# Layer norm boundaries by token halves: last two product units, statistics and first two product units of the next matrix

## The reference, cut to what matters

```
h = layer_norm(x, ln_in_g, ln_in_b)
for l in range(2):
    proj = h @ w_in[l]
    ...
    mix = jnp.concatenate([o_a, o_b, o_c, o_d], axis=-1) @ w_out[l]
    h = layer_norm(DEEPNORM_ALPHA * h + mix, ln_mix_g[l], ln_mix_b[l])
    up = depthwise_conv(h @ ffn_w_up[l], ffn_conv_w[l], ffn_conv_b[l])
    f = (jax.nn.silu(up[..., :D_FF]) * up[..., D_FF:]) @ ffn_w_down[l]
    h = layer_norm(DEEPNORM_ALPHA * h + f, ln_ffn_g[l], ln_ffn_b[l])
return h

def layer_norm(x, g, b):
    mu = jnp.mean(x); var = jnp.mean((x - mu) ** 2)
    return (x - mu) * lax.rsqrt(var + 1e-5) * g + b
```

## Time and profile before

| | us |
|---|---|
| median of 3 runs | 2164.02 (2162.97 to 2166.41) |
| span of the profiled execution | 2162.8 |
| around the span, to the median | 1.2 |
| TensorE busy | 2072.4 (96%) |
| VectorE busy | 1186.1 (55%) |
| ScalarE busy | 786.0 (36%) |
| GpSimd busy | 176.5 (8%) |
| mean granted TensorE clock | 0.986 |

### The profile page before, as it was taken

The page is one execution under the profiler, slowest core; times in us unless marked ns, Lnnn a source line. Parts: engine busy times, 40 slices in busy tenths (PEclk is TensorE's granted clock), DMA queues, the critical chain, the costliest instruction groups (busy, mean ns, idle before and its releaser), DMA issues.

```text
span 2162.8 us, 24857 instructions
## 1 busy us (share of the span) xinstructions
PE 2072.4 (96%) x10090; PEld 1444.9 (67%) x10090; DVE 1186.1 (55%) x1798; ACT 786.0 (36%) x1199; POOL 176.5 (8%) x132
## 2 busy tenths in 40 slices
PE   6999999999999889889999999999999999999997
PEld 4787788843333333348657788888776677888885
DVE  6556534423333233366885864656677858646565
ACT  4546533312211111144673421222345734212233
POOL 1000000010000000000100110102001001101020
PEclk9999999999999999999999999999999999999999
DMA  5342243499999999942202222232222022222221
GB/s 193 117 150 75 78 175 116 157 359 408 406 408 400 398 410 415 421 153 79 72 1 78 90 95 97 87 101 98 96 100 71 2 78 96 95 97 87 101 95 52
DMA packets 41137, 357.61 MB, mean 165 GB/s; under 512 B 6320, under 2 KB 7512, under 8 KB 13376
## 3 DMA queue, kind: packets, MB, share of 16 engines
q1 hardware_dynamic: 36448, 342.99, 41.6%
q0 software_dynamic: 4288, 10.95, 1.7%
q10 hardware_dynamic: 288, 2.10, 0.2%
HBM read 354.94 MB, written 6.83 MB: 167 GB/s over the span
## 4 chain that ended last, share of the span: by engine, by line
PE 81%; DMA 9%; DVE 4%; ACT 3%; issue 2%; SPq 0%; DVEq 0%; ACTq 0%
PE bank L1103 40%; PE bank L2093 10%; PE bank L458 8%; DMA H<-in_expert_up_w 5%; PE bank L473 3%; PE bank L480 2%; DMA AUX<-in_expert_up_w 2%; DMA ring<-in_expert_up_w 2%; PE bank L1885 2%; PE bank L1870 1%; PE bank L1901 1%; PE bank L2118 1%; PE bank L1130 1%; PE bank L2186 1%; ACT S L1950 1%
## 5 line engine op out<-in xcount | busy, mean ns | idle before, releaser
L1103 PE MATMUL bank<-split_x_high,split_weights 128*128 128x512 f32 x1888 | 586.4, 390 | 0.1
L1103 PEld LDWEIGHTS bank<-split_x_high,split_weights 128*128 128x128 f32 x1888 | 354.4, 188 | 76.8 <-issue 3.3
L1364 ACT ACTIVATE split_weights<-ring 128x2048 fp32r<-128x2048 f32 (+1 forms) x113 | 211.1, 1868 | 532.5 <-PE bank L1103 467.7
L1356 DVE TENSOR_TENSOR split_weights<-ring,split_weights 128x2048 fp32r<-128x2048 f32 (+2 forms) x115 | 258.5, 2248 | 164.5 <-ACT split_weights L1364 164.4
L1103 PE MATMUL bank<-split_products,split_weights 128*128 128x512 f32 x1136 | 302.7, 389 | 0.0
L1103 PE MATMUL bank<-split_x_low,split_weights 128*128 128x512 f32 x736 | 286.3, 389 | 0.0
L1103 PEld LDWEIGHTS bank<-split_products,split_weights 128*128 128x128 f32 x1136 | 213.2, 188 | 44.6 <-issue 0.5
L2093 PE MATMUL bank<-split_x_high,split_weights 128*128 128x512 f32 x480 | 153.4, 398 | 6.7 <-DVE split_x_low L2295 6.7
L1103 PEld LDWEIGHTS bank<-split_x_low,split_weights 128*128 128x128 f32 x736 | 138.2, 188 | 28.4
L1080 POOL TENSOR_TENSOR QKVG<-QKVG 128x512 f32<-128x512 f32 x44 | 97.9, 2224 | 551.9 <-DVE QKVG L1567 466.6
L686 DVE SCALAR_TENSOR_TENSOR S<-S,stats,bank 64x512 f32<-64x512 f32 x32 | 23.6, 739 | 197.0 <-ACT S L810 197.0
(11 more groups left out here) (469 smaller groups left out, 3206.6 us busy)
## 6 DMA issues: line engine op xcount, KB each, us to landing
ring<-in_ffn_w_up SPq DMA_DIRECT2D x44, 1024.0 KB, 4.8
ring<-in_w_in SPq DMA_DIRECT2D x24, 1024.0 KB, 4.8
QKVG<-in_expert_gate_w SPq DMA_DIRECT2D x11, 2048.0 KB, 26.4
AUX<-in_expert_up_w SPq DMA_DIRECT2D x11, 2048.0 KB, 31.0
QKVG<-in_expert_down_w SPq DMA_DIRECT2D x11, 2048.0 KB, 33.1
MKV<-in_expert_gate_w SPq DMA_DIRECT2D x11, 2048.0 KB, 30.3
ring<-in_expert_up_w SPq DMA_DIRECT2D x11, 2048.0 KB, 35.8
ring<-in_expert_down_w SPq DMA_DIRECT2D x11, 2048.0 KB, 27.9
```

Of the source, the lines that this page charges most:

```text
L1103: mm = pe.matmul(acc[:, :], w[:, u, k, m], x, start=first and q == 0, stop=last and q == 2)
L1356: st.tell(dve.tensor_tensor(w[:, 1, 0:ks, 0:nc_], raw_half(g)[:, :, 0:nc_], as_f32(w[:, 0, 0:ks, 0:nc_]), ALU.subtract), wl_done)
L1364: st.tell(act.activation(WHL[g % 2][:, 0, 0:ks, 0:nc_], raw_half(g)[:, :, 0:nc_], ACT.Copy), wh_done)
```

## The change

The two last units of each of the four ending products, the statistics, the scaling and the two first units of the next product are done for tokens 0 to 255 (h = 0) and then for tokens 256 to 511 (h = 1).

- `half_units`: units 2 and 3 of the ending product run as h0 unit 2, h0 unit 3, h1 unit 2, h1 unit 3, each 48 matmuls with 256 moving columns. Their two tiles share one bank. In front of them TensorE waits until the fourth full width tile has been added. The products by ones of half 0 stand behind the second of the last four tile products, that is between h1 unit 2 and h1 unit 3.
- `first_units`: the two first units of the next product run as h0 unit A, the products by ones of half 1, h0 unit B, h1 unit A, h1 unit B. The four products by ones that nothing reads are gone.
- The running sum of X moves from VectorE to GpSimd (`sums_and_centres`), at full width for chunks 1 to 3 and by halves for chunks 4 to 7, and GpSimd centres two pairs of chunks in each half.
- VectorE centres, scales and makes low parts for pairs of chunks by half (128 x 2 x 256) with tensor_tensor out of SBUF; g and b are both applied by ScalarE, which lays a pair as two XH and, behind a wait for them, two X. The low part now waits for both.
- The result leaves in eight stores of 256 KB in place of four of 512 KB.

```
...
+            def sums_and_centres(use, added):
+
+                for m in range(1, N_FULL):
+                    pool.wait_ge(r_free, added + m + 1)
...
+                for h in range(2):
+                    for j in range(2):
+                        pool.wait_ge(rh_free, 4 * use + 2 * h + j + 1)
+                        for m in (N_FULL + 2 * j, N_FULL + 2 * j + 1):
+                            st.wait()
+                            ins = pool.tensor_tensor(sum_x[:, TH[h]], sum_x[:, TH[h]], X[:, m, TH[h]], ALU.add)
+                            st.tell(ins, x_summed) if m == DC - 1 else st.do(ins)
+                    pool.wait_ge(ln_mean, 2 * (2 * use + h) + 1)
+                    for p in (2, 3):
+                        x = chunk_pair(p, h)
+                        st.tell(pool.tensor_tensor(x, x, both(sum_x, h), ALU.add), ln_pool)
...
+                def half_units(use, g, banks, ks, operands):
+
+                    for h in range(2):
+                        for j in range(2):
+                            pe.wait_ge(wl_done, g + j + 1)
+                            w, acc = WHL[(g + j) % 2], bank[banks[2 * h + j]]
+                            for i in range(2):
+                                for k in ks:
+                                    high, low = operands(k)
+                                    mm = three(acc[:, i * T // 2:(i + 1) * T // 2], w, slice(i * P, (i + 1) * P), k, high[:, TH[h]], low[:, TH[h]], k == ks[0], k == ks[-1])
+                                if h == 1 and j == 0 and i == 1:
+                                    stat(use, 0)
+                            mm.then_inc(rh_done, 1)
...
-                layernorm(2 * l, 7, 5, l * NR_DONE + DC, 4)
...
+                pe.wait_ge(r_free, l * NR_DONE + 4)
+                half_units(2 * l, g + 1, (0, 1, 2, 3), order, lambda k: (XH[:, k, :], OL[k]))
+                first_units(2 * l, UA + l * NU + NF, [bank[i] for i in range(4)], XL, f_done)
...
+                variance(0)
+                residual(1, 0)
                 if low:
-                    dve_x_low(dve, st, use + 1, low, bias, DC - 1)
+                    unit_low(dve, st, unit)
+                scale(0, 0)
+                scale(0, 1)
+                low_part(0, 0)
+                scale(0, 2)
+                low_part(0, 1)
+                scale(0, 3)
+                add_half_squares(use, 1, 0)
+                residual(1, 1)
+                low_part(0, 2)
+                low_part(0, 3)
+                add_half_squares(use, 1, 1)
+                if low:
+                    unit_low(dve, st, unit + 1)
+                variance(1)
...
+                def laid(h, p):
+                    act.wait_ge(ln_scaled, (2 * use + h) * (DC // 2) + p + 1)
                     if split:
...
+                        for c in (2 * p, 2 * p + 1):
+                            st.tell(act.activation(XH[:, c, TH[h]], X[:, c, TH[h]], ACT.Identity, bias=b(c), scale=g(c)), xh_done)
+                        st.wait()
+                    for c in (2 * p, 2 * p + 1):
+                        st.tell(act.activation(X[:, c, TH[h]], X[:, c, TH[h]], ACT.Identity, bias=b(c), scale=g(c)), ln_ready)
...
```

388 lines of the change are left out of this document (218 added, 170 removed).

## The result

The changed kernel took 2208.68 us (median of 4, 2208.12 to 2209.72) where the kernel before took 2165.02 beside it (2162.97 to 2166.41): 1.0204 times the time before, 95% interval 1.0189 to 1.0218. The forecast was 2189.9 with a range of 2170 to 2200. The sign was right and the price was not: +43.6 us between the two profiled spans (2206.4 and 2162.8) against +25.9.

The account below looks back on a forecast made before the run. TensorE, busy 96% of the span, was taken as the bound; stalls at three boundaries added +20.4 us and the end +5.5, together +25.9 on 2164.0, giving 2189.9 us, range 2170 to 2200.

Parts of the forecast that it names:

- TensorE's work: At each boundary, eight half width units of 48 matmuls cost 46.1 us where four full ones cost 43.5: +2.6 us.
- The stall in front of half 0: TensorE waits 3.48 us for the first XH of half 0, starting the next product's first unit at 28.41.
- One lock: VectorE and GpSimd operations on SBUF take turns at a shared port, so centring, scaling and low parts wait for GpSimd's additions.
- rival (a): The port costs less than assumed: without turns boundaries take 56.4, 55.0, 56.4, the end -0.1; 2171 us, chance 0.17.
- The end's 6.3 us: At the program's end, the last products by ones start 6.3 us after the last matmul, behind VectorE's late last residual.
- Rival (c): Faster: XH comes before TensorE asks and ScalarE keeps step, -14.1 at three boundaries, 2149.8 us; chance 0.05.
- Rival (d): Sums not under cover: GpSimd's 256 wide additions take 1.3 us, half 1's products by ones 1.2 later; +5, 2195; chance 0.06.
- side estimate of 4.3 us: By the skill's 0.109 us per 256-column matmul, a boundary would be 4.3 us shorter (384 matmuls); the row's 0.120 was used.
- residual wait 0.97: In front of the half units TensorE waits 0.97 us for the residual of the tile it has just finished.
- Rival (b): TensorE's clock falls inside the boundary behind the 3.5 us stall: +2.3 a boundary, +7, 2197 us; chance 0.18.
- 4 x 0.40: ScalarE's pace per pair of chunks: four operations at 0.40 plus a wait of 0.16, 1.76 us against TensorE's 1.44.
- the floor of 48.9: TensorE's least time per boundary: residual wait 0.97, half units 46.1, products by ones 1.84; 4.7 us less than before.

Follow-up runs that it names:

- the run with both engines nearly free: Changed kernel with squares first, centring out of PSUM, reordered end, and GpSimd's half width work and ScalarE's final X on 8 columns: 2168.95 us, ratio 1.0014.
- the run that filled it: Changed kernel with four unread products by ones inside the residual's wait at the two down boundaries: 2202.27 us, ratio 1.0169.
- the run with the small X: Changed kernel with ScalarE writing only 8 of 256 columns of each final X: 2196.28 us, ratio 1.014.
- the fastest order by halves: Changed kernel with squares first, centring out of PSUM, reordered end, g on VectorE, low part waiting for XH only: 2177.74 us, ratio 1.006.

## Why the prediction was right in sign and wrong in size

**What held.** TensorE's work: 48 matmuls of 256 columns in 5.76 us, and the residual's wait at the mixing boundaries. The stall in front of half 0: TensorE starts at 28.20 and 28.21 where the account said 28.41, and at the down boundary too once its wait and clock are taken off. "One lock": L1484 0.94, L1475 1.78; without GpSimd's work the stretches are 4.6, 2.9, 4.0 and 3.9 shorter, where rival (a) had put 4.5 a boundary. (With the clock's 0.7 taken out of the first, and the 1.1 that a longer fall behind the residual's wait cost in the second added, all are 3.9 to 4.0.) The end's 6.3 us in front of the last sums were 5.88. Rival (c) had no chance: even the run with both engines nearly free does not reach 53.6. Rival (d) is out too: GpSimd's 256 wide additions take 0.85 each, beside VectorE's sums of squares, and not 1.3; the account had 0.68, which moved nothing, since the sums of half 0 were ready early.

```profile
1170.01 1.70 POOL L1085 TENSOR_TENSOR nothing<-nothing,X 128x256 f32<-128x256 f32 x2 [5.50 <-DVE X L1653]
```

The side estimate of 4.3 us in the prediction's paragraph on TensorE's work is 4.2 by its own two figures; nothing rests on it.

**What failed**, of 43.6 - 25.9 = 17.7 us:

1. The term "residual wait 0.97" was taken from the mixing boundary and used at all four. At the two down boundaries it is 4.06, through two queues: 2 x 3.1 us. I had listed what is queued behind the new wait, and not what stands in front of the instruction that releases it.
2. The clock behind that wait: 1.3 and 1.4 us by the run that filled it, 1.1 and 1.2 of it over my account (28.54 against 27.44 at the second boundary, 31.51 against 30.33 at the end), together 2.3. Rival (b) looked for the fall behind the stall for XH and put 2.3 us on each boundary. It fell there too, but half 0 hides it, and a second fall in half 1 cost 0.7 us at the first boundary and nothing at the third; most of its price is paid where TensorE alone is the bound behind the wait.
3. ScalarE's pace. The term "4 x 0.40" came from operations with a bias only, by width alone, and the changed kernel gives them a bias and a scale: 0.50. From XH of half 0 to XH of half 1 it is +1.05 us at each of three boundaries, from there to the third unit +1.83, +1.32 and +1.18: together 7.5 us, of which 0.7 at the first boundary is the clock of half 1, so 6.8. In the run with the small X, where a pair takes 1.70 us, the first part is 17.04 (17.43 in the account) and the second 14.58, 13.33 and 15.22 (15.06, 13.66 and 15.06), so with about the assumed pace the account holds within 0.5 us. No run changes the 0.10 us by itself. The Trainium skill has this price, ScalarE: Activation LUTs, section "What ACT_TABLE_LOAD costs": a [128,1] pointer operand adds some 93 ns to an operation; by it the change's scale operand was to be charged, and 0.59 and 0.50 us against 0.50 and 0.40 (the run with g on VectorE, two in 0.90) agree.
4. The start of the second block, 1.9 us later in this profile, is the first block's own variation, no part of the change.

These are 6.2 + 2.3 + 7.5 + 1.9 = 17.9 (the 7.5 with the 0.7 of half 1's clock in it); with -0.4 in front of half 0 at the mixing boundaries, -0.2 behind the last sums and 0.4 between the stretches the 17.7 is accounted for. So nearly half of the miss (8.5) is one queue order at two places, and 6.8 the mis-sized pace of an engine that had been named as the bound.

**Why the idea costs time at all.** A boundary had 4.7 us to win over the floor of 48.9. In the fastest order by halves a stretch is still 57.7, 8.8 over that floor: 2.03 for XH, 0.90 for a low part, 1.04 for the sum of squares and 1.08 for the third unit are idle time, and behind the first of them eight matmuls take 1.70 us at the lower clock where 8 x 0.12 is their pace. The 8.75 us gap of before was dear to look at and cheap to have: without its four idle products it costs 0.1 to 0.8 us more, and nothing under it has to be split in two.

## What to carry to other kernels

When a change adds a wait, follow the releasing instruction back through its own engine's queue and the queues that feed it, at every place where the wait stands: the same code at another boundary had a weight copy in front of a square and cost 4.4 us instead of none. Price an operation by its operands as well as its width, and look again at an engine that has just become the bound, since there 0.1 us an operation is paid at each of 32 operations of a boundary. A fallen TensorE clock is worth filling above all where TensorE itself is what is waited for afterwards, since the unit's other waits are taken off its price.

## What the runs showed of the hardware

ScalarE's operations of 8 columns with scale and bias still take 0.29 to the next (1.08 and 0.68 for two), so narrow ones are mostly fixed cost. The TensorE clock fell to 0.50 in or just behind waits of 3.1 to 5 us, and in half 1 behind waits of 1.35 and 1.14 with eight matmuls between them; it stayed there for a little over 3 us in some places and nearly 7 in others, and the same code showed both lengths and, behind a wait of 1.53 for XH, both a fall and none. Four fp32 products in a wait kept it at 1.00. VectorE's L1484, one SBUF input and 256 columns, took 0.29 beside GpSimd operations of 8 columns, 0.45 beside full ones when the centring came out of PSUM, and 0.94 when it did not.
